# Later weight-sum loads, a statistic at the end of an up block, and regular spread copies in the gated FFN of a two-block transformer kernel

## The reference, cut to what matters

```python
h = rmsnorm(x, ffn_pre_norm[i])
f = (jax.nn.silu(h @ w_gate[i]) * (h @ w_up[i])) @ w_down[i]     # D_FF = 2816
x = x + rmsnorm(f, ffn_post_norm[i])
e = rmsnorm(p[i] @ w_ple_proj[i], ple_norm[i])
x = x + jax.nn.sigmoid(x @ w_ple_gate[i]) * e
...
bias = rel_bias[:, bidx].astype(jnp.float32)     # second block, attention
```

## Time and profile before

| what | value |
|---|---|
| median of 3 runs | 1959.2 us (1959.13 to 1962.45) |
| profiled execution, its own time | 1959.2 us |
| its span, first to last instruction | 1957.3 us |
| TensorE matmul busy | 1928.2 us, 99% of the span |
| VectorE, ScalarE, GpSimd busy | 63%, 46%, 27% |
| mean granted TensorE clock | 0.997 of full speed |

### The profile page before, as it was taken

How to read it: one execution, slowest core, us unless ns; L and a number is a source line. 1 busy time by engine, 2 the same in 40 slices (tenths; PEclk the granted TensorE clock), 3 DMA queues, 4 the chain that set the end, 5 groups by cost and what they waited for, 6 DMA issues and landing times.

```text
span 1957.3 us, 23729 instructions
## 1 busy us (share of the span) xinstructions
PE 1928.2 (99%) x9278; PEld 1607.2 (82%) x9278; DVE 1229.2 (63%) x1697; ACT 898.3 (46%) x1309; POOL 537.4 (27%) x396
## 2 busy tenths in 40 slices
PE   8999989999999999999999999999999999999998
PEld 7877868888888888888888888888888888888886
DVE  7667755628335854545456857667666676866758
ACT  7445543424235452524245534434455555444435
POOL 2333634151324435353533000000333341000000
PEclk9999999999999999999999999999999999999999
DMA  5312247576571322222225456464322225746453
GB/s 164 94 44 76 98 93 160 151 121 155 112 124 62 112 86 86 87 86 86 86 78 158 118 183 171 130 172 121 115 85 85 86 65 178 177 129 172 122 180 86
DMA packets 164690, 229.70 MB, mean 117 GB/s; under 512 B 4784, under 2 KB 108976, under 8 KB 164464
## 3 DMA queue, kind: packets, MB, share of 16 engines
q1 hardware_dynamic: 146912, 192.61, 29.9%
q0 software_dynamic: 16096, 32.01, 9.5%
q10 hardware_dynamic: 1584, 3.74, 3.8%
HBM read 223.23 MB, written 4.72 MB: 116 GB/s over the span
## 4 chain that ended last, share of the span: by engine, by line
PE 93%; DVE 3%; ACT 2%; DMA 1%; issue 0%; POOL 0%; SPq 0%; ACTq 0%; DVEq 0%
PE ps L1143 29%; PE ps L1145 29%; PE ps L1144 29%; PE ps L1315 1%; PE ps L1345 1%; DMA raw<-in_w_gate 1%; PE ps L1354 1%; PE ps L1355 1%; PE ps L1332 1%; ACT scr L2247 0%; ACT w_hi L2000 0%; PE ps L1847 0%; DVE x L3246 0%; DVE hn_lo L3250 0%; DMA raw<-in_w_in 0%
## 5 line engine op out<-in xcount | busy, mean ns | idle before, releaser
L1143 PE MATMUL ps<-hn_hi,w_hi 128*128 128x512 f32 (+1 forms) x1556 | 608.8, 391 | 13.0 <-POOL w_lo L1043 8.1
L1145 PE MATMUL ps<-hn_hi,w_lo 128*128 128x512 f32 (+1 forms) x1556 | 600.2, 386 | 0.0
L1144 PE MATMUL ps<-hn_lo,w_hi 128*128 128x512 f32 (+1 forms) x1556 | 599.9, 386 | 0.0
L997 POOL TENSOR_TENSOR w_lo<-raw,w_hi 128x512 fp32r<-128x512 f32 x244 | 343.8, 1441 | 519.9 <-ACT w_hi L1992 519.9
L1143 PEld LDWEIGHTS ps<-hn_hi,w_hi 128*128 128x128 f32 x1556 | 293.2, 188 | 76.1 <-issue 14.2
L1145 PEld LDWEIGHTS ps<-hn_hi,w_lo 128*128 128x128 f32 x1556 | 292.8, 188 | 59.3
L1144 PEld LDWEIGHTS ps<-hn_lo,w_hi 128*128 128x128 f32 x1556 | 293.3, 189 | 57.8 <-issue 1.4
L1143 PE MATMUL ps<-w_hi,hid_hi 128*128 128x512 f32 x616 | 240.0, 390 | 0.1
L1144 PE MATMUL ps<-w_lo,hid_hi 128*128 128x512 f32 x616 | 239.7, 389 | 0.0
L1145 PE MATMUL ps<-w_hi,hid_lo 128*128 128x512 f32 x616 | 239.6, 389 | 0.0
L2036 ACT ACTIVATE w_hi<-raw 128x1024 fp32r<-128x1024 f32 x112 | 116.1, 1055 | 205.9 <-PE ps L1145 205.6
(11 more groups left out here) (383 smaller groups left out, 2905.9 us busy)
## 6 DMA issues: line engine op xcount, KB each, us to landing
raw<-in_mlp_w SPq DMA_DIRECT2D x56, 1024.0 KB, 5.4
raw<-in_ret_w_in SPq DMA_DIRECT2D x24, 1024.0 KB, 5.1
aux<-in_mlp_w POOLq DMA_DIRECT2D x16, 1024.0 KB, 9.0
raw<-in_att_w_in SPq DMA_DIRECT2D x12, 1024.0 KB, 5.3
raw<-in_w_gate SPq DMA_DIRECT2D x11, 1024.0 KB, 5.3
raw<-in_w_up SPq DMA_DIRECT2D x11, 1024.0 KB, 7.7
raw<-in_w_down SPq DMA_DIRECT2D x9, 1024.0 KB, 6.5
raw<-in_ret_w_out SPq DMA_DIRECT2D x8, 1024.0 KB, 5.0
```

The lines of the kernel that those rows point to most:

```text
L997: ins = pool.tensor_tensor(w_lo[:, slot, at], raw[:, slot, at], w_hi[:, slot, at].bitcast(F32), ALU.subtract)
L1143: pe.matmul(o, hi, rhs_hi, start=start, stop=False, skip_group_check=True)
L1144: pe.matmul(o, hi, rhs_lo, start=False, stop=False, skip_group_check=True)
L1145: return pe.matmul(o, lo, rhs_hi, start=False, stop=stop, skip_group_check=True)
```

## The change

1. The load of S3 into `aux` moves from behind the load of up block 3 to behind load 8 (A11). In group 0 it waits there for the statistic of `N_PLE` (`norm_stat`); A21's first half waits for `post_x`, long reached, and no longer for the statistic.
2. The squares and the halves of `N_PLE` move from `tmp` to the first half of `aux`.
3. GpSimd issues the addition for S3 after the `w_lo` of all eight up blocks, and no longer after that of block 5.
4. On TensorE the statistic and the columns move from the middle of up block 7 to the end of up block 6.
5. The spread copies are issued two per block pair in all four pairs of groups 0 and 1; group 2 has none.

```diff
-                    if g < 2 and j == 3:
-                        if g == 0:
-                            sp.wait_ge(s["apart_sum"], 2)
-                        else:
-                            sp.wait_ge(s["w_lo_ready"], FFN.ready(0, FFN.down(0, FFN.S4), 1))
-                        sp.dma_start(s3_m_s4..., w_down[g, 1, 0]).then_inc(s["s3_in"], 16)
...
                 load_ffn_raw(g, 8, w_down[g, 0, 0], 4)
                 if g == 0:
                     sp.wait_ge(s["norm_stat"], N_PLE.index + 1)
                 else:
+                    sp.wait_ge(s["w_lo_ready"], FFN.ready(0, FFN.down(0, FFN.S4), 1))
+                sp.dma_start(s3_m_s4..., w_down[g, 1, 0]).then_inc(s["s3_in"], 16)
+                load_ffn_raw(g, 9, w_down[g, 1, 0], 4)
+                if g == 0:
+                    sp.wait_ge(s["post_x"], 2 * KD)
+                else:
                     sp.wait_ge(s["w_lo_ready"], FFN.ready(0, FFN.down(0, FFN.A21), 0))
-                load_a21(g, 0)
-                load_ffn_raw(g, 9, w_down[g, 1, 0], 4)
-                load_ffn_raw(g, 10, w_down[g, 1, 1], 4)
-                sp.wait_ge(pair_free[1], FFN.taken_pair(g, 3, 1))
-                load_a21(g, 1)
+                for half in range(2):
+                    if half:
+                        sp.wait_ge(pair_free[1], FFN.taken_pair(g, 3, 1))
+                    sp.dma_start(ffn_a21[half]..., w_down[g, 0, 1, ...]).then_inc(s["a21_in"], 16)
+                    if half == 0:
+                        load_ffn_raw(g, 10, w_down[g, 1, 1], 4)
...  GpSimd
             for b in range(8):
                 ffn_up_lo(0, b, parts=b == 2)
-                if b == 5:
-                    ffn_s3(0)
-            ffn_s1_s4(0)
+            ffn_weight_sums(0)       # the addition for S3, then those for S1 and S4
...  TensorE
-                    elif (g, b) == (0, 7):
-                        ffn_up(g, b, range(4), stop=False)
-                        for half in range(2):
-                            stat_halves(N_PLE, half, tmp_halves)
-                        ffn_r_columns()
-                        ffn_up(g, b, range(4, KD), start=False)
                     else:
                         ffn_up(g, b, range(KD))
+                    if (g, b) == (0, 6):
+                        for half in range(2):
+                            stat_halves(N_PLE, half, aux_halves)
+                        ffn_r_columns()
...  ScalarE, groups 0 and 1
-                            square(N_PLE, t, e_buf[:, t, :], tmp)
-                    if j < 3:
-                        for n in range(2 * j, min(2 * j + 2, 5)):
-                            spread_ext(5 * g + n)
+                            square(N_PLE, t, e_buf[:, t, :], aux[:, 0:2, :])
+                    for n in range(2):
+                        spread_ext(8 * g + 2 * j + n)
...  ScalarE, group 2
-                for n in range(2):
-                    spread_ext(10 + 2 * j + n)
```

More of the change, by code:

```diff
@@ L444, in build @@
         tab = sb("tab", [P, 2, S])
+        aux_at = nc.sbuf_base
         aux = sb("aux", [P, 4, S])
@@ L450, in build @@
         sq_halves = nc.alloc_sbuf_tensor_at("sq_halves", (P, 2, S), F32R, offset=scr_at + S * 4)
-        tmp_halves = nc.alloc_sbuf_tensor_at("tmp_halves", (P, 2, S), F32R, offset=scr_at + 3 * S * 4)
+        aux_halves = nc.alloc_sbuf_tensor_at("aux_halves", (P, 2, S), F32R, offset=aux_at)
         gains = sb("gains", [P, N_GAINS])
@@ L848, in _ @@
                 load_ffn_up(0, j)
-            def load_a21(g, half):
-                sp.dma_start(ffn_a21[half].rearrange("p (k c) -> p k c", k=2),
-                             w_down[g, 0, 1, :, 2 * half:2 * half + 2, :]).then_inc(s["a21_in"], 16)
             for g in range(3):
@@ L856, in _ @@
                     load_ffn_up(g, j)
-                    if g < 2 and j == 3:
-                        if g == 0:
-                            sp.wait_ge(s["apart_sum"], 2)
-                        else:
-                            sp.wait_ge(s["w_lo_ready"], FFN.ready(0, FFN.down(0, FFN.S4), 1))
-                        sp.dma_start(s3_m_s4.rearrange("p (k c) -> p k c", k=4), w_down[g, 1, 0]).then_inc(s["s3_in"], 16)
                 if g == 2:
@@ L871, in _ @@
                 else:
-                    sp.wait_ge(s["w_lo_ready"], FFN.ready(0, FFN.down(0, FFN.A21), 0))
-                load_a21(g, 0)
-                load_ffn_raw(g, 9, w_down[g, 1, 0], 4)
-                load_ffn_raw(g, 10, w_down[g, 1, 1], 4)
-                sp.wait_ge(pair_free[1], FFN.taken_pair(g, 3, 1))
-                load_a21(g, 1)
+                    sp.wait_ge(s["w_lo_ready"], FFN.ready(0, FFN.down(0, FFN.S4), 1))
+                sp.dma_start(s3_m_s4.rearrange("p (k c) -> p k c", k=4), w_down[g, 1, 0]).then_inc(s["s3_in"], 16)
+                load_ffn_raw(g, 9, w_down[g, 1, 0], 4)
+                if g == 0:
+                    sp.wait_ge(s["post_x"], 2 * KD)
+                else:
+                    sp.wait_ge(s["w_lo_ready"], FFN.ready(0, FFN.down(0, FFN.A21), 0))
+                for half in range(2):
+                    if half:
+                        sp.wait_ge(pair_free[1], FFN.taken_pair(g, 3, 1))
+                    sp.dma_start(ffn_a21[half].rearrange("p (k c) -> p k c", k=2),
+                                 w_down[g, 0, 1, :, 2 * half:2 * half + 2, :]).then_inc(s["a21_in"], 16)
+                    if half == 0:
+                        load_ffn_raw(g, 10, w_down[g, 1, 1], 4)
                 for j in range(2):
@@ L1048, in ffn_up_lo, with ffn_weight_sums @@
                         ins.then_inc(s["w_part"], 1)
-            w_down = T["w_down"][0, 0:2048, :].rearrange("(g a k p) (f c) -> g a f p k c", g=2, a=2, p=P, f=2)
-            def ffn_s3(g):
+            def ffn_weight_sums(g):
+                w_down = T["w_down"][0, 0:2048, :].rearrange("(g a k p) (f c) -> g a f p k c", g=2, a=2, p=P, f=2)
                 s3 = s3_m_s4.rearrange("p (k c) -> p k c", k=4)
@@ L1056, in ffn_s3 @@
                 pool.dma_start(s3, w_down[g, 1, 1], accum_op=ALU.add).then_inc(s["s3_added"], 16)
-            def ffn_s1_s4(g):
-                s3 = s3_m_s4.rearrange("p (k c) -> p k c", k=4)
                 slot = FFN.raw_slot(g, FFN.load_s1(g))
@@ L1075, in _ @@
                 ffn_up_lo(1, b)
-                if b == 5:
-                    ffn_s3(1)
-            ffn_s1_s4(1)
+            ffn_weight_sums(1)
             pool.wait_ge(s["w_lo_ready"], FFN.ready(2, 0, 1))
@@ L2852, in sums @@
                     dve.wait_ge(s["norm_acc"], norm.acc0 + norm.n - 1)
-                    halves = tmp_halves if norm is N_PLE else sq_halves
+                    halves = aux_halves if norm is N_PLE else sq_halves
                     dve.tensor_copy(halves[:, 0, :], ssq).then_inc(s["norm_acc"], 1)
@@ L3359, in _ @@
                             if g == 0 and t:
-                                sums(N_PLE, t, tmp)
+                                sums(N_PLE, t, aux[:, 0:2, :])
                             if g == 1:
```

## The result

The changed kernel takes 1981.85 us (median of 4 runs, 1980.21 to 1982.42) where the kernel before took 1960.35 on the same chip: a ratio of 1.0107 [1.0090, 1.0125]. It is slower, by 1.07%. The profiled execution took 1980.7, with a span of 1978.8, 21.5 more than before.

The account below looks back on a forecast made before the run. TensorE, busy 1928.2 of 1957.3 us, was taken as the bound, so new waits show in full. -9.95 + 3.6 + 12.7 + 1.9 + 5.7 + 1.9 = +15.9 gave span 1973.2, forecast 1975 us, range 1956 to 1985.

Parts of the forecast that it names:

- The gap: TensorE's wait before up block 4 of group 0 (282.47 to 290.53) and its low clock go: -9.95 us.
- The statistic: End of up block 6, group 0: TensorE waits for VectorE's halves, then block 7's load is late: +3.6 us (2.1 to 6.6).
- block 7's weights: Group 0: their load, behind the copies of j = 1, lands 0 to 4.5 us late; 1.5 taken.
- Group 0's down part: S3's addition meets the pair of j = 3, S3 late by 10.7 us: +12.7 (4.1 to 14.6), +1.9 for clock.
- VectorE's chain behind S3: Group 0's down part: VectorE is slower than TensorE from S3 to S1, so 2.0 us more are paid.
- Group 1's down part: S3 loaded in time, M late behind A21's second half: +5.7 us (0 to 9.3), clock +1.9 (0 to 1.9).
- The A21 mechanism: Group 1: A21's second half lands behind the pair of j = 3, at +38, making M 5.1 us late.
- the other side: Rival (b): by queue turns, an addition in flight could be through a few us earlier.
- (a): Rival: only group 0 is held up, group 1's loads come in time; +8.2, 1961 to 1967 us; chance 0.20.
- (b): Rival: copies don't hold up the additions; -3.8 to -2.2, 1955.4 to 1957 us, or 1953; chance 0.24.
- (c): Rival: pairs also delay A12 by over 3 us and block 7's weights, both groups at upper bounds; +24.4, 1983.6; chance 0.10.
- (d): Rival: the gap at 282 us stays, block 4's load late for another reason; +26, 1985 us; chance 0.02.

Follow-up runs that it names:

- copies 6/6/4: The changed kernel without spread copies at j = 3, pairs kept at j = 0, 1, 2 of groups 0 and 1, four copies in group 2: 1965.94 us, 1.0028.

## Why the prediction was right, and where it was off

The forecast was 1975, slower, in a range that ends at 1985; measured were 1981.85. The sign held, and so did the cause, pairs of copies that hold up what the down parts need. Two terms were too small, the statistic's and group 1's, and in group 1 the sum put the wait at the wrong block.

**The gap: -9.95, measured -9.6,** and 10.4 in the run that has this part alone. Block 4's load left at 263.46, as worked out from GpSimd's run (262.6), and landed in 5.3 us.

**The statistic: +3.6, measured +6.1.** The idle time was right (2.1 forecast, 2.3 measured). The term of 1.5 us for block 7's weights was not: that load landed 13.6 us after its issue and about 0.3 us late. What was missed is the clock. I had priced it only behind long gaps; here 2.3 us of idle time with the eight small matmuls behind them brought TensorE to 1.2 GHz for 6.9 us. The run without the small matmuls there, same idle time, kept 2.4 GHz; the wait of 1.27 us in the earlier trace rows, with large matmuls behind it, cost no clock either. That it takes both, idle time and small matmuls, is shown for this place only: in the run with copies 6/6/4, 2.26 us of idle time with large matmuls behind them led to 1.2 GHz as well, and 2.97 us in the same run did not.

**Group 0's down part: +14.6 with the clock, measured +14.3.** The steps in order: S3's load landed at +27.0 from the end of block 5 (forecast +27.1), A12 at +29.7 (+29.9), and S3's addition at +49.1, where I had +44.5 and had given +46.3 as the upper end. S3 was 11.5 late, not 10.7. That these agree is luck in good part. The landing was 4.6 too early in the sum, and TensorE's arrival at S3 3.8 (+36.2 for +40.0), 2.5 of it the statistic's and some 1.4 a slip: block 7's end at +25.3 leaves out the matmuls of the statistic and the columns, with which it had ended at +23.2 before (337.73 - 314.56). VectorE's chain behind S3, counted at 2.0, cost only 0.5.

The row for this was at hand. I priced the addition by the quiet one, 8.7 us; S3's own additions of 16.6 and 13.8 us in the same trace had stood behind a pair.

**Group 1's down part: +7.6 with the clock, measured +10.7.** This is the step that failed in its mechanism. I had S3 in time and M late behind A21's second half. In the trace S3's addition was issued at +8.3 (forecast +8.5) and took 30.0 us. I had put its turn ahead of the loads behind it, because it was issued first; the trace shows that it came behind them (below). The A21 mechanism exists: it is the wait of 6.66 in the run with one copy at j = 2. It only stood behind a longer one. A21's second half landed at +41.1, the late end of what I gave; with my +38.1 for TensorE and 5.2 us from the sum to M's `w_lo`, M would have been some 8 us late by itself, an estimate.

**Why an addition takes 30 us.** At first it stands still. The queues from 461 to 470 us of the changed kernel (packets, MB, share of 16 engines), behind the pair of j = 2 of group 1 that was issued at 457.47:

```profile
q10 hardware_dynamic: 114, 0.24, 88.3%
q1 hardware_dynamic: 9, 0.02, 0.5%
```

q10 carries the spread copies, q1 the loads of SyncE and q0 the additions, which has no packet here at all. The addition was issued at 460.23, and its first packet falls between 472.0 and 472.5; A12's load was issued 0.07 us behind it, and its first packet falls between 469.5 and 470.0. Group 0 shows the same. S3's load, issued at 319.10 behind the pair of 315.78, has its first packet between 328.0 and 328.5. S3's addition, issued at 332.30 while loads fill the engines, has it between 337.0 and 337.5. With nothing else in flight an addition has its first packet about 2 us after its issue (353.94 in the kernel before: 355.5 to 356.0). So what was issued behind a pair waited until the pair was nearly through, and the addition waited for loads as well. Why it starts last the trace doesn't show.

Once it moves, it crawls. From 340 to 348 us, with the pair of j = 3 of group 0 in flight:

```profile
q10 hardware_dynamic: 105, 0.23, 83.0%
q0 software_dynamic: 103, 0.21, 17.9%
q1 hardware_dynamic: 104, 0.20, 7.7%
```

All three queues move the same number of packets: here they take turns, one for one. But a packet of a copy keeps its engine for long. 83% of sixteen engines for 8 us are 106 engine-us, 1.0 for each of the 105 packets; for q0 it is 0.22 and for q1 0.09. While the pair moves, the addition gets one packet per packet of a copy, 0.21 MB in 8 us. The Trainium skill (DMA: Bandwidth & Descriptors, Queues, rings and completion order) says that each DMA engine goes round its queues and changes at packet boundaries. The equal counts agree with it; the 12 us in which the addition was issued and moved nothing show no such turns. I had cited that rule for the other side, as a help to the addition. In this stretch the turns are the same in count, not in time, and only what is already moving has them.

One for one isn't general. In the kernel before, from 276 to 284 us, a pair was in flight beside up-block loads with packets of 1 KB and not 2, and the loads moved more than three packets per packet of a copy:

```profile
q10 hardware_dynamic: 119, 0.25, 86.3%
q1 hardware_dynamic: 388, 0.39, 13.7%
```

The 30.0 us of group 1 are thus about 12 of standing still, 7 of turns with the loads (to 479), and 11 with the second pair.

The pairs of j = 2 and j = 3 are 17.4 us apart in group 1 (457.47 and 474.90). An addition that is to land between them has to be quick, and this one is caught by both. In the run with it 1.7 us earlier, counted from the end of block 5, it landed after 21.6 us, at 481.7, and the second pair, held back by the late A12, was issued at 481.99.

**The rivals.** (a), group 1 not held up, is out by 8.3 us of wait. (b), additions not held up, is out: 21.7 and 30.0 us. (c) came nearest in size, 1983.6, by upper bounds, of which group 1's held and that for block 7's late weights did not. (d) is out. (c) should have had a larger chance: both groups have the same cause, so it was likely that both would fare badly at once.

**What stays open.** Why runs of one kernel (one copy at j = 2) fall in two groups 6 to 9 us apart; why an addition moves no packet behind a pair or behind loads; what decides, beside the idle time, whether the clock falls; and about 2 us of the difference between the sum of the parts and the whole in single runs, which is near what the runs can tell.

## What to carry to other kernels

Price a background transfer by the time for which it holds the engines, not by its bytes: pairs of 160 KB copies, with the loads that they held up, delayed a megabyte by 13 us (one pair in flight) to 21 us (caught by two). Before two edits are put together, list what each takes away as cover: the moved sums and statistic together won 6 us here, the new copies alone cost 4, and all together cost 21.5. Take the price of a transfer from its own row in the trace, not from a quiet one of the same size. And when a gap has one cause, move only that: one number in one line (S3's load two blocks later) was worth 11 us.

## What the runs showed of the chip that I had not expected

- Two spread copies, 160 KB in 80 packets each, filled the DMA engines to 85.5% while they moved 0.32 MB in 12 us (316 to 328). An accumulating transfer of 1 MB beside one or two such pairs and other loads took 20.9 to 30.0 us instead of 8.7, a load of 1 MB behind a pair 12.9 instead of 5.2.
- A transfer issued behind a pair moved no packet for 9 us (the load of 319.10) and 12 us (the addition of 460.23). Transfers already moving when a pair came went on: one packet per packet of a copy (340 to 348), or three of half the size (276 to 284 in the kernel before).
- 2.3 us of idle time with eight 128x1 matmuls behind them led to 6.9 us at 1.2 GHz; the same idle time without these matmuls behind it led to none. Elsewhere 2.26 us of idle time led to 3.4 us at 1.2 GHz without them.
- A half megabyte issued 3.75 us ahead of a pair landed in 7.6 us. Those issued 0.01 to 0.02 us ahead of one landed in 4.2, 8.1, 9.9, 15.2 and 17.3 us, with different other transfers in flight.
